# Held rows scattered into a dead DRAM buffer and gathered over all eight prompt tiles

## The reference, cut to what matters

```python
h2 = rmsnorm(x, g_ffn).reshape(B * L, D_MODEL)
x = x + hier_moe(h2, w_grp, w_exp, w1, w3, w2).reshape(B, L, D_MODEL)
...
def run_block(args):          # one block of up to 128 rows of one expert
    tok, w, e = args
    xb = h[tok]
    a = jax.nn.silu(xb @ w1[e]) * (xb @ w3[e])
    return ((a @ w2[e]).astype(jnp.float32) * w[:, None]).astype(h.dtype)
...
y_prompt = rmsnorm(yp, g_final)      # over each token's 1024 columns
y_sample = rmsnorm(ys, g_final)
```

## Time and profile before

| | |
|---|---|
| Median of 3 runs | 1015.94 us (1015.56 to 1016.12) |
| The profiled execution | 1020.83 us, span 1019.1 us |
| PE busy | 967.0 us (95%) |
| DVE busy | 743.3 us (73%) |
| ACT busy | 440.6 us (43%) |
| POOL busy | 231.2 us (23%) |

### The profile page before, as it was taken

One profiled execution on the slowest core, in us unless ns is written; L12 is line 12 of the kernel. 1 busy time (PEld: TensorE's weight loads), 2 busy tenths in 40 slices (PEclk: granted clock), 3 DMA queues, 4 the chain that ended last, 5 costly groups with the idle time before them and its releaser, 6 DMA issues. The chain is left out here.

```text
span 1019.1 us, 16163 instructions
## 1 busy us (share of the span) xinstructions
PE 967.0 (95%) x5358; PEld 837.5 (82%) x5359; DVE 743.3 (73%) x1627; ACT 440.6 (43%) x736; POOL 231.2 (23%) x236
## 2 busy tenths in 40 slices
PE   6999999999999999999999999969999999999980
PEld 6998898988889888898886888858888888888860
DVE  5965467855658455685558765589999999999985
ACT  6621122121220111301213122138888988988964
POOL 0001220012200122001221110032434434443332
PEclk9999999999999999999999999979999999999995
DMA  9511105111051110511218342289999999999956
GB/s 316 180 42 54 41 22 175 41 53 38 26 173 32 50 45 21 177 39 36 80 35 283 149 153 97 105 307 410 395 388 394 400 393 387 397 394 384 360 204 244
DMA packets 76323, 191.59 MB, mean 188 GB/s; under 512 B 13712, under 2 KB 48828, under 8 KB 63827
## 3 DMA queue, kind: packets, MB, share of 16 engines
q1 hardware_dynamic: 61355, 159.10, 41.4%
q0 software_dynamic: 14752, 31.03, 10.0%
q10 hardware_dynamic: 144, 0.52, 0.1%
HBM read 172.70 MB, written 38.68 MB: 207 GB/s over the span
## 5 line engine op out<-in xcount | busy, mean ns | idle before, releaser
L1409 DVE TENSOR_TENSOR w_lo<-w,w_hi 128x1024 fp32r<-128x1024 f32 x128 | 150.5, 1218 | 0.3
L832 ACT ACTIVATE w_hi<-w 128x1024 fp32r<-128x1024 f32 x128 | 129.5, 1069 | 3.3 <-PE bank L946 3.3
L944 PE MATMUL bank<-w_hi,xT_hi 128*128 128x512 f32 x256 | 102.9, 402 | 2.4 <-issue 2.2
L2158 PE MATMUL bank<-wvg_hi,hT_hi 128*128 128x512 f32 x256 | 104.3, 408 | 0.0
L2513 POOL TENSOR_TENSOR mixed<-onorm,pgate 128x256 f32<-128x256 f32 x36 | 39.0, 1082 | 275.8 <-DVE onorm L2329 275.8
L2158 PE MATMUL bank<-wvg_lo,hT_hi 128*128 128x512 f32 x256 | 100.9, 394 | 0.0
L2158 PE MATMUL bank<-wvg_hi,hT_lo 128*128 128x512 f32 x256 | 100.7, 393 | 0.0
L946 PE MATMUL bank<-w_hi,xT_lo 128*128 128x512 f32 x256 | 100.2, 391 | 0.0
L945 PE MATMUL bank<-w_lo,xT_hi 128*128 128x512 f32 x256 | 99.7, 390 | 0.0
L1965 ACT ACTIVATE v<-bank 128x256 f32<-128x256 f32 x32 | 12.3, 383 | 201.2 <-PE bank L2159 201.2
L944 PE MATMUL bank<-hT_hi,wuqk_hi 128*128 128x344 f32 x288 | 94.8, 329 | 0.1
(11 more groups left out here) (300 smaller groups left out, 2408.2 us busy)
## 6 DMA issues: line engine op xcount, KB each, us to landing
w<-in_w_dram SPq DMA_DIRECT2D x96, 1024.0 KB
raw<-in_w_in_dram SPq DMA_DIRECT2D x57, 256.0 KB, 3.4
mixed_d<-mixed POOLq DMA_DIRECT2D x32, 128.0 KB, 2.2
sample_state<-in_state_ret_dram SPq DMA_DIRECT2D x16, 256.0 KB, 3.8
out_dram<-sample_state SPq DMA_DIRECT2D x16, 256.0 KB, 3.5
mixed_in<-mixed_d SPq DMA_DIRECT2D x8, 512.0 KB, 4.3
x_again<-in_x_prompt_dram SPq DMA_DIRECT2D x8, 512.0 KB, 3.5
h_d<-h POOLq DMA_DIRECT2D x8, 512.0 KB, 3.0
```

The costliest lines, as they stand in the source:

```text
L832: act.activation(hi, whole_w, ACT.Copy).then_inc(S["up_hi"], 1)
L944: pe.matmul(out, lhs[0], rhs[0], start=first, stop=False)
L1409: dve.tensor_tensor(lo, whole_w, hi, ALU.subtract).then_inc(S["up_lo"], 1)
L2158: g = pe.matmul(gates, x[xi], wvg[wi][:, 1:3, k, :], start=first, stop=last)
```

## The change

The held rows are scattered into `mixed_d` instead of `sum_d`. `OVER` becomes all eight prompt tiles, `ORDER` becomes CH, 0 to 7. SP loads all eight tiles and the samples' rows from `sum_d` early; POOL's scatters no longer wait for those loads; the gathers over the tiles read `mixed_d`, and there are eight of them. The samples' short rows are joined by DVE from two loads: `fin_s` (the early one) and `held_s` (from `mixed_d`), with a flag for each short row in `keep`, which PE spreads from `held_rows` with the matrix `spread`. The spilled block, skipped here, first brings the held rows back to `sum_d` and at its end to `mixed_d` again. The diff, without the changes inside the spilled block:

```diff
...
         gfin_s = nc.alloc_sbuf_tensor_at("gfin_s", [SR, SC], F32, offset=at_s + 4 * SC)
         same_row = nc.alloc_sbuf_tensor_at("same_row", [SR, NB, 8], F32, offset=at_s + 8 * SC)
         row_of = nc.alloc_sbuf_tensor_at("row_of", [SR, NB], F32, offset=at_s + 12 * SC)
+        held_s = nc.alloc_sbuf_tensor_at("held_s", [SR, SC], F32, offset=at_s + 16 * SC)
+        spread = nc.alloc_sbuf_tensor_at("spread", [NB, NB, 8], F32, offset=at_s + 20 * SC)
+        keep = nc.alloc_sbuf_tensor_at("keep", [SR, 2], F32, offset=at_s + 24 * SC)
 
         SS, MS, RS = 0, 9, 18
         TX = 36
...
             return xg_in[slot], 16 * (MAIN_USES[slot] + 2 + n // HELD)
 
         SQ2, SQ3, ROOT2, ROOT3 = NT + 1, 2 * NT + 1, 5, 5 + NT
-        AGAIN = (CH, 0, 1)
-        OVER = tuple(t for t in range(CH) if t not in AGAIN)
-        ORDER = (CH, 0, 2, 1, 3, 4, 5, 6, 7)
+        OVER = tuple(range(CH))
+        ORDER = (CH,) + OVER
         NORM_GROUPS = ((0, 2), (2, 4), (4, 6), (6, 9))
         GAINS = 16 * (2 + NB)
 
...
             for i in range(2):
                 sp.wait_ge(sum_out[i], SUMS[i])
             for t in OVER:
                 sp.dma_start(fin[:, t, :], sum_d[t * P:(t + 1) * P, :]).then_inc(rows_in[t], 16)
+            sp.dma_start(fin_s[:, :], in_parts(sum_d[SEQ:NTOK, :])).then_inc(rows_in[CH], 16)
             for r in range(NB):
                 sp.dma_start(gfin_s[8 * r:8 * r + 8, :], g_final.rearrange("(i c) -> i c", c=SC)).then_inc(gains_in, 16)
             spilled(sp, more, tiles_landed, tiles_again)
 
 
             sp.wait_ge(z_out, 16 * HELD)
-            sp.dma_start(fin_s[:, :], in_parts(sum_d[SEQ:NTOK, :])).then_inc(rows_in[CH], 16)
-            for t in (0, 1):
-                sp.dma_start(fin[:, t, :], sum_d[t * P:(t + 1) * P, :]).then_inc(rows_in[t], 16)
+            sp.wait_ge(rows_in[CH], 48)
+            sp.dma_start(held_s[:, :], in_parts(mixed_d[SEQ:NTOK, :])).then_inc(rows_in[CH], 16)
             for n, t in enumerate(ORDER):
                 dst = y_prompt[0, t * P:(t + 1) * P, :] if t < CH else in_parts(y_sample.rearrange("b o d -> (b o) d"))
                 for half in halves_of(n):
...
                 if t in OVER:
                     act.wait_ge(*held_in(t))
                 else:
-                    act.wait_ge(rows_in[t], 48 if t == CH else 32)
+                    act.wait_ge(S["z_done"], after(HELD + 1))
                 act.wait_ge(S["sq_done"], after(squares_before(n)))
                 act.activation(junk_f[r, 0:tile_of(n).shape[1]], tile_of(n), ACT.Square, scale=D ** -0.5,
                                accum_out=small[r, SS + n:SS + n + 1]).then_inc(S["sq_done"], 1)
                 if n == 1:
-                    act.wait_ge(S["l_mm"], after(NT + 1))
+                    act.wait_ge(S["l_mm"], after(NT + 2))
                     act.activation(small[0:SR, SS:SS + 1], banks[4][0:SR, 0:1], ACT.Copy).then_inc(S["sq_done"], 1)
                 for a, b in NORM_GROUPS:
                     if b == n + 1:
...
 
             spilled(pe, more, spill_start)
             pe.wait_ge(S["rows_known"], after(2))
+            pe.matmul(banks[4][0:SR, 1:2], spread[:, :, :].rearrange("p r i -> p (r i)"), held_rows[0:NB, CH:NT],
+                      start=True, stop=True).then_inc(S["l_mm"], 1)
             pe.wait_ge(S["sq_done"], after(SQ3 + 1))
             pe.matmul(banks[4][0:SR, 0:1], same_row[:, :, :].rearrange("p r i -> p (r i)"), small[0:SR, SS:SS + 1],
                       start=True, stop=True).then_inc(S["l_mm"], 1)
...
                 st.do(dve.scalar_tensor_tensor(
                     out=row_pair[:, :], in0=misc[:, TILE:TILE + 2 * NT:2], scalar=2.0 * P,
                     in1=misc[:, PAIR:PAIR + 1].to_broadcast([P, NT]), op0=ALU.mult, op1=ALU.add))
-                st.do(dve.tensor_scalar(held_rows[:, :], held_rows[:, :], -8192.0, 8192.0, ALU.mult, ALU.add))
-                st.do(dve.tensor_tensor(row_pair[:, :], held_rows[:, :], row_pair[:, :], ALU.add))
+                st.do(dve.tensor_scalar(held[:, 0:NT], held_rows[:, :], -8192.0, 8192.0, ALU.mult, ALU.add))
+                st.do(dve.tensor_tensor(row_pair[:, :], held[:, 0:NT], row_pair[:, :], ALU.add))
                 dve.tensor_scalar(row_held[:, :], row_pair[:, :], 1, None, ALU.logical_shift_right)\
                     .then_inc(S["rows_known"], 1)
 
...
                 dve.wait_ge(S["down_used"], after(4 * (NE - HELD + 1)))
                 st.do(dve.tensor_reduce(row_of[:, :], misc[0:SR, IDENT:IDENT + SR].rearrange("p (r i) -> p r i", i=8),
                                         AX, ALU.add))
+                dve.tensor_copy(spread[:, :, :], misc[0:NB, IDENT:IDENT + NB].unsqueeze(2).to_broadcast([NB, NB, 8]))
                 dve.tensor_copy(same_row[:, :, :], row_of[:, :].unsqueeze(2).to_broadcast([SR, NB, 8]))\
                     .then_inc(S["rows_known"], 1)
 
...
                 for q in range(DOWNS):
                     down_low(b, 0, q)
 
-            spilled(dve, more, spill_list)
+            def sample_rows():
+
+                dve.wait_ge(S["l_mm"], after(NT + 1))
+                dve.tensor_copy(keep[:, 0:1], banks[4][0:SR, 1:2])
+                do(dve.tensor_scalar(keep[:, 1:2], banks[4][0:SR, 1:2], -1.0, 1.0, ALU.mult, ALU.add))
+                dve.wait_ge(rows_in[CH], 48)
+                do(dve.tensor_scalar(fin_s[:, :], fin_s[:, :], keep[:, 1:2], None, ALU.mult))
+                dve.wait_ge(rows_in[CH], 64)
+                dve.scalar_tensor_tensor(out=fin_s[:, :], in0=held_s[:, :], scalar=keep[:, 0:1], in1=fin_s[:, :],
+                                         op0=ALU.mult, op1=ALU.add).then_inc(S["z_done"], 1)
+
+            spilled(dve, more, spill_list, lambda: dve.wait_ge(gains_in, GAINS + 16 * NT))
+            sample_rows()
 
 
 
...
                 pool.indirect_dma_start(out=xg[b % SLOTS][:, :], out_offset=None, in_=sum_d,
                                         in_offset=indexed(idx_tok[:, b:b + 1]),
                                         bounds_check=last_row, oob_is_err=False).then_inc(xg_in[b % SLOTS], 16)
-            for t in OVER:
-                pool.wait_ge(rows_in[t], 32)
+            def rows_back(b, d):
+                pool.indirect_dma_start(out=d, out_offset=indexed(idx_tok[:, b:b + 1]),
+                                        in_=xg[b % SLOTS][:, :], in_offset=None,
+                                        bounds_check=last_row, oob_is_err=False).then_inc(z_out, 16)
+
             for i, b in enumerate(range(NE - HELD, NE)):
                 pool.wait_ge(S["z_done"], after(i + 1))
-                pool.indirect_dma_start(out=sum_d, out_offset=indexed(idx_tok[:, b:b + 1]),
-                                        in_=xg[b % SLOTS][:, :], in_offset=None,
-                                        bounds_check=last_row, oob_is_err=False).then_inc(z_out, 16)
+                rows_back(b, mixed_d)
 
             def more(b, i):
                 pool.wait_ge(S["xt2_mm"], after(2 * b))
...
+            spilled(pool, more, held_to_sums, spill_sums)
             pool.wait_ge(S["rows_known"], after(1))
             pool.wait_ge(z_out, 16 * HELD)
             for t in OVER:
                 landed, count = held_in(t)
                 pool.wait_ge(landed, count - 16)
-                pool.indirect_dma_start(out=fin[:, t, :], out_offset=None, in_=sum_d,
+                pool.wait_ge(rows_in[t], 32)
+                pool.indirect_dma_start(out=fin[:, t, :], out_offset=None, in_=mixed_d,
                                         in_offset=indexed(row_held[:, t:t + 1]),
                                         bounds_check=last_row, oob_is_err=False).then_inc(landed, 16)
 
```

More of the change, by code:

```diff
@@ L762, in tiles_again @@
                     sp.dma_start(fin[:, t, :], sum_d[t * P:(t + 1) * P, :]).then_inc(gains_in, 16)
+                sp.dma_start(fin_s[:, :], in_parts(sum_d[SEQ:NTOK, :])).then_inc(gains_in, 16)
             for i in range(2):
@@ L1691, in more @@
                 gather(b, 0, MAIN_USES[0] + i + 1, icol[0][:, :])
-                pool.wait_ge(z_out, 16 * HELD)
-                carried(pool, "pool")
                 scatter(b, 0, None, icol[0][:, :])
@@ L1696, in more, with held_to_sums @@
                 carried(pool, "pool")
-            def spill_sums():
+            def held_to_sums():
+                pool.wait_ge(z_out, 16 * HELD)
+                for t in OVER:
+                    pool.wait_ge(rows_in[t], 32)
+                pool.wait_ge(rows_in[CH], 48)
+                for b in range(NE - HELD, NE):
+                    rows_back(b, sum_d)
+                pool.wait_ge(z_out, 32 * HELD)
+            def spill_sums():
+                for b in range(NE - HELD, NE):
+                    pool.indirect_dma_start(out=xg[b % SLOTS][:, :], out_offset=None, in_=sum_d,
+                                            in_offset=indexed(idx_tok[:, b:b + 1]), bounds_check=last_row,
+                                            oob_is_err=False).then_inc(z_out, 16)
```

(8 more changed lines are left out.)

## The result

The changed kernel is slower: 1019.67 us against 1016.82 us, medians of 11 runs each on one chip; ratio 1.0032, 95% interval [1.0018, 1.0046]. Run once more it gave 1019.84 against 1017.19, ratio 1.0026 [1.0011, 1.0041]. I had forecast 1013.6, 0.23% faster.

What follows compares the result with a forecast made beforehand. The end was taken as bound by when the first two tiles arrive, after scatters and gather, unless a later tile comes late. Last group and end move -2.3 us: median 1015.94 to 1013.6, range 1012.9 to 1014.0, with rivals 1 to 3 up to 1015.0.

Steps and rivals of the forecast that it cites:

- (a): Before POOL's scatters: dropping the wait for early `fin` loads starts the first at 989.1 instead of 990.31; gain 1.1 us.
- rival 2: Early loads did not hold the first scatter, so dropping POOL's wait gains nothing: -1.2 us, 1014.7; chance 0.12.
- (b): SP's queue: tiles 0 and 1 and the samples' rows load early, 1.08 MB more, ending near 992; costed at nothing.
- rival 3: The larger early-load backlog delays POOL's gathers into `xg` by 2.9 us: sum -0.9, 1015.0; chance 0.10.
- (c): The scatters' landing moves from 995.45 to 994.3, POOL's first gather from 996.27 to 995.15.
- (e): Samples' rows: `held_s` lands at 996.6, ACT can square at 997.0, ahead of tile 0, so the join costs nothing.
- (d): POOL's first gather, no longer behind 1 MB of direct loads, takes 2.5 us instead of 5.72; tile 0 lands at 997.65.
- (f): ACT squares tile 0 2.4 us earlier; DVE's second group starts 2.8 us earlier, at 1001.95.
- rival 4: Gather latency stays 5.72 us, so POOL's window of three delays gathers: +4.8, 1020.7; needs over 4.1 us; chance 0.05.
- (g): Eight gathers at 1.31 us spacing; tile 5 stalls ACT 0.5 us; DVE's last group at 1008.9 instead of 1011.22, -2.3.
- Rival 1: Stores hold the last gathers longer, a full store's 1.4 us at tile 5 or 7: -1.4 us, 1014.5; chance 0.15.
- (h): The end stays 7.9 us behind DVE's last group and shifts whole with it: -2.3 us.

## Why the prediction was wrong

(a) *POOL's wait*: right, and worth a little more than I said. First and third scatter came 1.6 and 1.3 us earlier on the mean, and the run with the wait put back shows the early loads as releaser; rival 2 is out. I had POOL need 0.8 us after DVE's rows; it needed 0.27 (982.99 to 983.26). And the third scatter is held by DVE after all: it starts 0.28 us behind the third rows (985.87 to 986.15), where I had POOL's own spacing as the limit.

(b) *Early loads at nothing*: half wrong. They ended about when I said (the last landed at +16.2 in the run with the wait put back, forecast +16), and DVE's row sums kept their time (the third done at +15.2 against +15.1, first profiles), so rival 3 is out as I put it. But the scatters' data met them in the engines (from +14 to +15 of the second profile q1 moved 0.19 MB beside q0's 0.12; in the kernel before q1 had nothing to move from +13.3 to +19): their landing gained 0.6 us on the mean, not 1.1. The cover that I named protected the gathers into `xg`, not the scatters.

(c), (e) The order of events was right, and the join of the samples costs nothing: DVE's 0.37 us and ACT's square at +21.0 and +21.2, forecast +21.0, ahead of tile 0.

(d) *The latency of a gather*: mis-sized. With nothing but SP's 32 KB load in the other queue it is 3.3 us (the first gather of the changed kernel 3.25 and 3.28, of the run with DVE held 3.36), where I took the scatter's 2.5 as nearest. 0.8 us on the first square, by which (f) shrank too. I also took 0.06 MB as a tile's data, from the earlier trace rows; all eight gathers move 0.79 MB, 0.1 MB each. The latency stays under the 4.1 us of rival 4, whose place (POOL's window of three) hardly held: in the run with DVE held the sixth gather came 0.18 us late by it, in that with the gain in PSUM none did. (In (f), 1.97 less 0.45 is 1.52 and not 1.54; it was 1.60.)

(g) *Eight gathers at the 1.31 us spacing*: this is the step that failed and made the change a loss. I took POOL's 1.0 us per gather as its own, from a trace in which gathers and scalings hardly met. The change adds two gathers and at the same time brings DVE's second group 1 us forward, so that two of the eight start under a scaling; these two then take 0.8 to 1.0 us more on POOL, their data falls behind further stores, and the last group comes at +36.5 where a stall of 0.5 us had it at +32.9. Without the stretching it comes at +34.3, so 2.2 us of the miss of 3.7 are this step's. Rival 1 had the right place and part of the cause: holding the stores back gave 1.6 us of the last group's start, but the stores without the stretching cost some 0.4 us, about my 0.5. The row that could have warned me is the earlier trace rows: 1003.74 took 1.14 us where its neighbours took 1.00, and DVE was ending a scaling at that moment. It ended at 1003.99, 0.89 us before the gather's end at 1004.88:

```profile
1002.72 1.27 DVE L1583 SCALAR_TENSOR_TENSOR fin<-fin,small,gfin_b 128x1024 f32<-128x1024 f32 x1
```

(h) held: the end followed the last group by 7.86 us in both profiles of the changed kernel, 7.88 and 7.82 in those of before.

Even with that mended, no gain shows: the version with the gain in PSUM has its first group at +24.6 and its last at +34.3, the kernel before 24.9 to 25.6 and 34.2 to 35.2. Of the 1.3 us that the scatters gain, the added loads take 0.7 on the mean. Tile 0 then comes only 0.3 us quicker than before: by a gather of 3.3 us, issued 0.8 us behind SP's load, for a direct load of 3.7 to 4.0 us, issued 0.6 us behind it. And with the gain in PSUM ACT still waits 0.41 and 0.34 us for late gathers.

## What to carry to other kernels

When a change moves work of one engine in time, look at which other engine's instructions it will now run beside, not only at what it waits for. Indirect DMAs issued by POOL are POOL's work, and a vector instruction with both operands in SBUF that runs at their start held them up by up to 1.1 us here; put one operand in PSUM, or keep the two apart. Replacing two large direct loads by two small gathers saves bytes on the path but spends POOL's issue time (1.31 us each here) and a latency of 3.3 us, with which the gathers overlap.

## What was not expected of the hardware

- A gather by POOL that starts under a 1.27 us scaling of DVE with two SBUF operands takes up to 2.10 us on POOL instead of 1.00, and ends 0.87 to 0.90 us after the scaling; with one operand in PSUM it takes 1.00. One that starts just ahead of or with the scaling is not held (the seventh gather of the second profile of the changed kernel, 1.00 us, beside a scaling that began 0.02 us earlier); one that starts 0.05 us behind it is held in full (the 2.10 us, with the gathers over tiles 0 and 1 left out).
- A gather of some 0.1 MB (0.79 MB for eight) lands 3.3 to 3.6 us after its start with no large load or store beside it; an indirect scatter of some 0.26 MB (0.79 MB for three) lands in 2.6. Why the smaller one takes longer stays open.
